# The first mixer's last columns wait for one weight unit each, and the blocks beside its heads change places

## The reference

```python
p = h @ w_in                                   # 1024 x 2568: gates, output gate, memory queries, q, k, v
q, k, v, o, gates, mq = split(p)
scores = (q @ k.T) * exp(dmat - m_row)          # each of 4 heads, each row tile of 128 tokens
hm = (scores @ v) / max(|sum(scores)|, exp(-m_row))
hm = sigmoid(o) * rmsnorm(hm) * g_out
mo = softmax(mq @ mk.T) @ mv                    # 4 memory heads
x = x + rmsnorm(concat([hm, mo]) @ w_out) * g   # then the feed-forward part, and further layers
```

## Time and profile before

| | |
|---|---|
| median of 3 runs | 2215.6 us (2213.72 to 2216.07) |
| the profiled execution's own time | 2219.75 us |
| its span, first to last instruction | 2218.3 us |
| PE busy | 2085.8 us, 94% of the span |
| PE's weight loads (PEld) busy | 1700.6 us, 77% |
| DVE busy, ACT busy | 1162.8 us (52%), 867.0 us (39%) |
| mean granted clock of PE | 0.973 of full speed |

### The profile page before, as it was taken

The page is one execution under the profiler, slowest core; times in us unless marked ns, Lnnn a source line. Parts: engine busy times, 40 slices in busy tenths (PEclk is TensorE's granted clock), DMA queues, the critical chain, the costliest instruction groups (busy, mean ns, idle before and its releaser), DMA issues.

```text
span 2218.3 us, 24613 instructions
## 1 busy us (share of the span) xinstructions
PE 2085.8 (94%) x9984; PEld 1700.6 (77%) x9984; DVE 1162.8 (52%) x2252; ACT 867.0 (39%) x1553; POOL 242.5 (11%) x185
## 2 busy tenths in 40 slices
PE   6999999999997999999999998999999799999797
PEld 6987788887876777788887888877777566877575
DVE  5425553332236565453333226998974428766553
ACT  5435542222232455442222213467552223366520
POOL 1001110000011000010000003677700000000000
PEclk9999999999998998999999999999999899999998
DMA  6320122223323211222332232322223212211211
GB/s 231 103 96 31 67 86 95 95 95 105 114 78 112 76 55 71 95 86 96 98 103 102 83 107 95 98 77 92 77 85 109 81 57 76 76 39 39 76 57 57
DMA packets 28800, 192.60 MB, mean 87 GB/s; under 512 B 3264, under 2 KB 3408, under 8 KB 7440
## 3 DMA queue, kind: packets, MB, share of 16 engines
q1 hardware_dynamic: 24848, 175.96, 23.3%
q0 software_dynamic: 3264, 12.99, 1.7%
q10 hardware_dynamic: 576, 2.10, 0.2%
HBM read 186.84 MB, written 4.19 MB: 86 GB/s over the span
## 4 chain that ended last, share of the span: by engine, by line
PE 80%; DVE 13%; ACT 5%; issue 1%; DMA 0%; POOL 0%; SPq 0%; DVEq 0%; ACTq 0%; POOLq 0%
PE bank L398 23%; PE bank L400 22%; PE bank L399 22%; DVE bank L2121 5%; PE bank L1807 2%; DVE WL L370 2%; PE bank L1698 1%; PE bank L1795 1%; ACT WH L356 1%; PE bank L1708 1%; PE bank L2262 1%; PE bank L1273 1%; PE bank L1184 1%; PE bank L543 1%; PE bank L1800 1%
## 5 line engine op out<-in xcount | busy, mean ns | idle before, releaser
L398 PE MATMUL bank<-XH,WH 128*128 128x512 f32 (+1 forms) x1504 | 596.3, 397 | 15.7 <-DVE XL L559 10.3
L400 PE MATMUL bank<-XH,WL 128*128 128x512 f32 (+1 forms) x1504 | 566.9, 377 | 0.0
L399 PE MATMUL bank<-XL,WH 128*128 128x512 f32 (+1 forms) x1504 | 566.4, 377 | 0.0
L370 DVE TENSOR_TENSOR WL<-RAW,WH 128x2048 fp32r<-128x2048 f32 x128 | 293.2, 2292 | 453.0 <-ACT WH L356 452.9
L356 ACT ACTIVATE WH<-RAW 128x2048 fp32r<-128x2048 f32 x148 | 282.3, 1908 | 329.2 <-PE bank L400 323.5
L398 PEld LDWEIGHTS bank<-XH,WH 128*128 128x128 f32 x1504 | 285.6, 190 | 85.4 <-issue 25.6
L399 PEld LDWEIGHTS bank<-XL,WH 128*128 128x128 f32 x1504 | 285.9, 190 | 55.0 <-issue 6.6
L400 PEld LDWEIGHTS bank<-XH,WL 128*128 128x128 f32 x1504 | 285.1, 190 | 53.1 <-issue 0.6
L2121 DVE SCALAR_TENSOR_TENSOR bank<-conv_in,cols,bank 128x512 f32<-128x512 f32 x290 | 198.3, 753 | 1.1
L398 PE MATMUL bank<-WH,XH 128*128 128x428 f32 (+2 forms) x416 | 159.5, 383 | 11.4 <-DVE XL L559 6.3
L399 PE MATMUL bank<-WL,XH 128*128 128x428 f32 (+2 forms) x416 | 154.6, 372 | 0.0
(11 more groups left out here) (333 smaller groups left out, 2990.2 us busy)
## 6 DMA issues: line engine op xcount, KB each, us to landing
RAW<-weights SPq DMA_DIRECT2D x164, 1024.0 KB, 4.8
row_a<-rows POOLq DMA_DIRECT2D x7, 512.0 KB, 5.9
row_b<-rows POOLq DMA_DIRECT2D x6, 512.0 KB, 6.1
x_res<-x SPq DMA_DIRECT2D x1, 2048.0 KB, 16.7
kv<-mem_park POOLq DMA_DIRECT2D x2, 1024.0 KB, 5.1
out<-x_res ACTq DMA_DIRECT2D x4, 512.0 KB, 2.6
mem_tok<-mem SPq DMA_DIRECT2D x1, 1024.0 KB, 4.9
mem_tok<-mem POOLq DMA_DIRECT2D x1, 1024.0 KB, 8.3
```

The lines of the kernel that those rows point to most:

```text
L370: dve.tensor_tensor(WL[j][:, :], RAW[j][:, :], WH[j][:, :].bitcast(F32), ALU.subtract).then_inc(*lo.mark())
L398: pe.matmul(ps, ah, bh, start=first, stop=False)
L399: pe.matmul(ps, ah, bl, start=False, stop=False)
L400: return pe.matmul(ps, al, bh, start=False, stop=last)
```

## The change

In the code of PE the four blocks of tile 0, b=0 of the last columns move ahead of the last key head's turn. The wait that stood in front of the first block, and asked for both units (`u + 2`, that is unit 11 too), becomes one wait for each unit, in front of the first block that uses it. In the table of the steps the last blocks of tile 3 (b=1) come at steps 16 to 19 instead of 21 to 24, the blocks of the next product for tile 0 at 20 to 23 instead of 17 to 20, those for tile 1 at 25 to 28 instead of 26 to 29. The quarters of unit out 1 are split at steps 21 to 24 instead of 26 to 29. `LAST_READY` follows from the table: ACT copies tile 3 of the last columns at step 20 instead of 25.

```diff
@@ in_a_pe
         in_a_unit_pe(4, 1)
+        for q in range(4):
+            last_columns_pe(0, 0, q)
         keys_turn_pe([2 * LH - 1])
@@ last_columns_pe
         u, kb = U["in_a", 2 * LAST + b], 4 * b + q
+        if q == 0:
+            PE.wait_ge("split_lo", u + 1)
         if kb == 0:
-            PE.wait_ge("split_lo", u + 2)
             take_bank("beside", "in_a", LAST, t)
@@ the table of the steps
     FIRST_FILL = {first + q: (what, t, b, q) for first, what, t, b in (
-        (0, "in_a", 1, 1), (4, "in_a", 2, 0), (8, "in_a", 3, 0), (12, "in_a", 2, 1), (17, "out", 0, 0), (21, "in_a", 3, 1),
-        (26, "out", 1, 0), (33, "out", 2, 0)) for q in range(4)}
+        (0, "in_a", 1, 1), (4, "in_a", 2, 0), (8, "in_a", 3, 0), (12, "in_a", 2, 1), (16, "in_a", 3, 1), (20, "out", 0, 0),
+        (25, "out", 1, 0), (33, "out", 2, 0)) for q in range(4)}
-    QUARTER_STEPS = {first + q: q for first in (13, 26) for q in range(4)}
+    QUARTER_STEPS = {first + q: q for first in (13, 21) for q in range(4)}
@@ mlstm_pe
-        for t, b in ((0, 0), (1, 0), (0, 1)):
+        for t, b in ((1, 0), (0, 1)):
             for q in range(4):
                 last_columns_pe(t, b, q)
```

## The result

The changed kernel takes 2203.41 us in the median of 5 runs (2200.71 to 2205.53); the kernel before took 2214.98 us beside it, also in 5 (2213.72 to 2216.07). The ratio is 0.9946 with a 95% interval of 0.9932 to 0.9961: 12.0 us less, with 8.6 and 15.1 as the ends. In a later comparison the changed kernel took 2206.36 us in 6 runs, and the kernel before 2222.54 in 11: 0.9935 (0.9916 to 0.9953). The prediction was 2205.1 us, 10.5 less than before. The profiled execution's own time is 2203.41 us, its span 2201.9, its mean granted clock 0.977 (before: 0.973).

What follows compares the result with a forecast made beforehand. PE bounds the kernel, busy 94% of the span with 80% of the last-ending chain. Gains of 5.9 and 5.1 less a 0.5 us new wait make 10.5, taking the 2215.6 median to 2205.1 us; range 2202.5 to 2209.0.

Steps and rivals of the forecast that it cites:

- The first place: Last key head's turn, behind group 4: tile 0's early blocks fill PE's idle time and keep the clock up, 5.9 us.
- The low clock and the slow turn: At the last keys' turn: 2.2 us saved from the 1.2 GHz stretch, 0.5 from the slow turn and what lay around it.
- S1: Start of group 4's last matmul to start of the last columns' 36th matmul: forecast 8.0 us instead of 13.9.
- The second place: Steps 16 to 19: ready blocks of unit 11 replace PE's waits for DVE, 5.1 us, before the new wait of 0.5.
- The term for the low clock: Behind the wait at step 17: full clock instead of a mean of 0.74 over 6.54 us, taken as 1.6 us saved.
- S2: Start of the last columns' 36th matmul to first matmul behind the heads; 79.80 us before, 75.25 in the changed kernel.
- The new wait at step 25: PE waits for tile 1's low part, delayed on DVE by quarters: some 0.5 us lost, from nothing to 1.3.
- the clock falls at the turn all the same: Rival at the last keys' turn: low clock and slow turns remain, 8.0 us gained, 2207.6 us; chance 0.12.
- DVE is the true bound: Rival at steps 16 to 25: the wait only moves, second gain at most 1 us, 2208.7 us; chance 0.09.
- the gain doesn't arrive: Rival: the change fails or a later stage takes it back, 0 to 4 us left, 2213.6 us; chance 0.06.
- Slower: Rival: PE waits for DVE at steps 22 to 25, clock stays low through the heads, 2232.8 us; chance 0.03.
- the kernel's own spread: Whole kernel: a spread of about 1 us, counted in the forecast's own range of 9 to 12 us gain.

Runs made afterwards that it cites:

- e4: Kernel before with one wait for each unit and no blocks moved; 2209.28 us, ratio 0.9969 to the kernel before.
- e3: Changed kernel, but the first early block waits for both units again; 2209.75 us, ratio 0.9993 to the kernel before.
- e5: Changed kernel with the quarters of unit out 1 back at steps 26 to 29; 2204.22 us, ratio 0.9939 to the kernel before.
- e8: Changed kernel with the last key head's four transposes done four times over; 2202.82 us, ratio 0.994 to the kernel before.
- e7: Changed kernel, DVE doing a tile's low part ahead of the quarter at the same step; 2205.82 us, ratio 0.9966 to the kernel before.
- e2: Kernel before with only the changed table of steps and quarters; 2214.16 us, ratio 0.9984 to the kernel before.
- e1: Kernel before with only the early blocks and separate waits at the last keys' turn; 2211.58 us, ratio 0.9979 to the kernel before.
- e6: Changed kernel with two of the four blocks ahead of the turn, two behind it; 2210.05 us, ratio 0.9967 to the kernel before.

## Why the prediction was right

**The first place: 5.9 predicted, 6.02 measured.** The turn stood 0.23 us idle (0.2 predicted), the pace was 0.195 us, the clock 1.00. The idle time fell by 3.10 us, which are the 2.36 of work put into the gap and the 0.76 of the wait. The low clock and the slow turn, 2.2 + 0.5, measured 2.92. S1 came out at 7.86 for 8.0, mostly because four transposes took 0.36 us and not the fifth part of twenty, 0.47. That a wait split alone would not have done it, and a move alone would have lost, is shown by e4 and e3.

**The second place: 5.1 - 0.5 = 4.6 predicted, 4.55 measured.** No wait for L391 at step 17; of the 1.08 us at step 16 I left 0.41, and by starts 0.41 is what stands there. The term for the low clock, 1.6, is the fall of PE's busy time in S2, 1.61. The new wait at step 25, 0.5, is 0.41; a wait of 0.27 us near the end of the heads left with the quarters, which the working named as small and didn't count, and e5 brings it back. I had called the early quarters a cost of 0.5; e5 puts the net at 0.27.

**The sum: 10.5 predicted, 10.57 in the place.** The medians gave 12.0 (8.6 to 15.1) and in the second comparison 0.65%, 14.4 us (10.4 to 18.7). 10.57 lies inside both. That the median itself came within 1.7 us of 2205.1 is partly luck: the medians of the kernel before alone lay between 2214.7 and 2222.5 us in the later groups of runs, and e8, with 1.3 us more of work, had the lower median. ACT's first split behind the mixer shows that nothing was given back on the way:

```profile
247.94 1.92 ACT L356 ACTIVATE WH<-RAW 128x2048 fp32r<-128x2048 f32 x1 [7.62 <-PE bank L400]
```

It still waits 7.62 us for PE, and it came 261.21 - 247.94 = 13.27 us earlier than in the earlier trace rows: 10.57 of the place and the 2.71 of chance ahead of it. The forecast of 10.5 for what follows the mixer is right net of that chance.

**The rivals.** That the clock falls at the turn all the same, 2207.6 us: 1.00 from the turn to the 36th matmul, in e8 even with sixteen transposes. The Trainium skill (TensorE: Matmul & The Clock Gate, Part 4: PE-mode transpose) says that the full clock doesn't come into play for transposes. The traces disagree in so far as these ran at a granted clock of 1.00 and didn't end it; whether transposes alone would raise the clock, no run shows. That DVE is the true bound: it is the bound of the remaining 0.25 and 0.41 us (e7), and of no more. That the gain doesn't arrive: the four rests, which both kernels have on one line, speak against it. Slower: PE waited at one of the steps 22 to 25, not at four, and no low clock followed.

**What was off.** The size of a low stretch. I costed it from one profile, as if it belonged to the stall before it. The two profiles of before agree on it, but in e4 the one was half as long and the other twice, and elsewhere the same stall was followed by the low clock in one execution of the changed kernel and not in another. So the terms of 2.2 and 1.6 us have no fixed price behind them. They came out because the low stretches had the same lengths again in the repeat of before and, each at its one place, in e2 and e1, and because the clock was up at both places in both profiles of the changed kernel. From the one profile that I had, that was luck. And I gave the kernel's own spread as 1 us; in the later runs the changed kernel alone went from 2197.13 to 2208.39.

## What to carry to other kernels

A wait that asks for two things in front of work that needs one is worth splitting only together with work that can use it: in S1 the split wait alone gave 2.16 us, of which 0.76 were idle time and 1.40 clock, while S2 grew by 1.31 of clock alone; the moved blocks alone lost 0.56; both together gave 6.02. At the two places each stall of 2.56 to 2.61 us was followed by a low clock, in all profiles that had one, and of the 10.57 us that went with the stalls 6.04 were idle time and 4.53 clock. The idle time is the part of a gain that can be counted on; the clock's part is read afterwards. And where medians scatter by 5 us, compare the stretch between two named instructions (here it repeated to within 0.04 us in both kernels), and take the time at the low clock off the rest.

## What the runs showed of the hardware

The granted clock can fall at a place where the profile has PE busy, and not in every execution. Of two profiles of the kernel before, the same stretch, first the one of the kernel before, then its repeat:

```profile
90.00:100.00 10.00, 10.00 (x54) 9.64 (x53) 5.79 (x5) 6.66 (x7) 0.00 (x0) 0.83 0.33 107
```

```profile
90.00:100.00 10.00, 10.00 (x60) 9.70 (x60) 5.80 (x5) 6.55 (x7) 0.00 (x0) 1.00 0.32 107
```

PE has no idle time in either; six matmuls fewer stand in the first, at 0.83. In both, though, a part of the busy time is light work: twenty matmuls of 4 columns each (L1032) fill 2.1 us, in the first profile from 90.69 to 92.84, and there the clock falls less than 1 us behind them: it is 0.50 from 93.50 to 96.90. Behind the heads stretches at the low clock made 5.2 and 6.5 us of difference between two executions of one program, half of what the change is worth.

By the four rests a microsecond at 1.2 GHz cost about 0.505 us. A half is what it costs where PE is the bound all the time, so PE was the bound in nearly all of it.

And the idle time ahead doesn't settle what the clock does. At the turn 1.40 us left it up (e6), and 2.57 us was followed by 0.50. But two stalls of 1.32 and 1.29 us were followed by some 10 us at the low level in one execution of the changed kernel and by none in the other, and a stall of 4.20 us by a low stretch of different length in two executions of the kernel before.
